# Gathered expert rows: products ahead of the preceding pair's sums, searches in four pieces, six row slots in place of eight

## The chip, the cores and the metric

The kernel runs on one core of a Trainium2 chip. The core has TensorE (PE, matrix products), VectorE (DVE), ScalarE (ACT), GpSimd (POOL) and SyncE (SP), each with an instruction queue of its own, and 16 DMA engines that they share. The metric is the device time of one execution in microseconds (us).

## What is computed

One layer of an encoder for 1024 tokens of width 1024, in float32: three mixers side by side (retention, gated unit, window attention), their merge, then a retrieval over 16384 experts (PEER), then a gated input embedding. The change lies in the retrieval and its surroundings. For a block of 128 tokens:

```python
q = (xt @ wq).reshape(T, PEER_HEADS, 2, PEER_QDIM // 2)          # 8 heads, two halves of 128
s = jnp.einsum('thpc,hpkc->thpk', q, kf)                         # 128 scores for each half
s1, i1 = lax.top_k(s[:, :, 0], 16)
s2, i2 = lax.top_k(s[:, :, 1], 16)
cand_s = s1[..., :, None] + s2[..., None, :]                     # 256 pairs
top_s, sel = lax.top_k(cand_s.reshape(T, PEER_HEADS, 256), 16)
eid = ...                                                        # i1 * 128 + i2 of the 16 chosen
gate = jax.nn.softmax(top_s, axis=-1)
act = jax.nn.gelu(jnp.einsum('thkd,td->thk', u_tab[eid], xt))
return jnp.einsum('thk,thkd->td', gate * act, v_tab[eid])
```

Each token picks 8 x 16 = 128 experts, and for each it needs one row u (1024 floats) and one row v (1024 floats). The kernel holds u and v side by side in one table, so an expert is a row of 8 KB.

## The kernel before

Two earlier stages (keys and branches) compute the mixers. The late stage, `late_stage` from line 969, merges them, projects, searches and retrieves. Tokens sit on the 128 partitions, one tile of 128 tokens at a time, 8 tiles. A "row" r of the code is one of the 1024 combinations of tile, head and chosen expert (8 x 8 x 16). For each row r, GpSimd issues one indirect DMA (`row`, lines 1186 to 1199) that fetches, for each of the 128 tokens, its own 8 KB table row: 1 MB in all. The tile `rows` in SBUF has SLOTS = 8 slots, and row r goes to slot r % 8. So GpSimd waits before gather r until row r - 8 has been summed.

What is done with a row:
- the product (`dot`, lines 1561 to 1569): VectorE multiplies u by the normalized input and adds up, one number per token;
- the weight (`weights`, line 1418): ScalarE applies GELU to the two products of a pair and multiplies by the gates; for rows of TensorE it also builds a diagonal matrix (line 1431);
- the sum (`weigh`): the v half times the weight is added to the tile's sum. Odd rows, and the even rows with r % 8 = 6, go to TensorE (`on_tensor`, line 824; product with the diagonal matrix, line 1297); the other even rows, 3 of 8, go to VectorE (line 1578).

The order of the work is written out ahead of time by the class `Plan` (line 838). It divides the late stage into slots of time, each with a list of jobs, and every engine runs through the slots in order. From the slot `first` on, each slot takes one pair of rows, 512 pairs in all. In slot s VectorE does first the merge jobs of slot s - 1, then the sums of pair s - 1 (which need ScalarE's weights), then the two products of pair s, then at the end of a tile the joining of the two sums (`finish`), and then the pieces of the searches that are planned for this slot. ScalarE does the evacuations of the jobs of slot s - 1 and then the weights of pair s. TensorE does its sums of pair s - 1 and then the jobs of slot s: projections of the next group of tiles, spread over the slots by their estimated times. They are there until tile 5 begins, and thin out as the groups of tiles end.

The searches for head q (the tile's heads in order) are planned by `searches` (line 950) in three pieces: both key searches (slot 3 of the group of 8 pairs that belongs to head q - 2), the search over the 256 pairs (slot 4) and the choice of experts (slot 6). One search (`top16`) is made of MAX8, FIND_INDEX8 and MATCH_REPLACE8 instructions. ScalarE converts indices (`convert`) in the slot after the pair search and scales the gates (`share`) in the slot after the choice. SP loads the scores of head q into one of two buffers in the slot in which head q - 2 has its pair search (line 1150).

Of the kernel before, what the change touches and what calls it, by code (L numbers as in the profile page):

```python
# [25 lines left out]
T = S // P  # L26
# [11 lines left out]
NSEL = PH * TOPK  # L38
# [7 lines left out]


FIRST = 1
SLOTS = 8


class Semaphores:
# [771 lines left out]
def on_tensor(r):  # L824

    return r % 2 == 1 or r % 8 == 6
# [11 lines left out]
class Plan:  # L838
# [111 lines left out]
    def searches(self):  # L950

        self.order = [(t, h) for t in range(T) for h in range(PH)]
        self.parts, self.part_slot = [[] for _ in range(self.n_slots)], {}
        ready = lambda q: self.of["scored", self.order[q][0], self.order[q][1] // 2].slot + 1

        def put(slot, q, part):
            assert slot >= ready(q), (slot, q, ready(q))
            self.parts[slot].append((q, part))
            self.part_slot[q, part] = slot

        for q in range(2):
            for part in range(3):
                put(self.first - 2 + (q + part + 1) // 2, q, part)
        for q in range(2, T * PH):
            for part, after in enumerate((3, 4, 6)):
                put(self.first + (q - 2) * HEAD_PAIRS + after, q, part)


def late_stage(nc, A, R, X):


    plan = Plan()
    with ExitStack() as ctx:
# [3 lines left out]
        K = max(len(g) for g in GROUPS)  # L977
        rows = sb("rows", [P, SLOTS, 2 * D])
        ring_rest = sb("ring", [P, RING - 2, CHUNK])
# [9 lines left out]
        s_in = sb("s_in", [P, 2, 2, PK])  # L989
        hot = sb("hot", [P, TOPK, 2, TOPK])  # L990
        top, top_at, top_f = sb("top", [P, 2, TOPK]), sb("top_at", [P, 2, TOPK], U32), sb("top_f", [P, 2, TOPK])
# [33 lines left out]
        xn_in, acc_in = [sem(f"xn{n}_in") for n in range(2)], [sem(f"acc{n}_in") for n in range(2)]  # L1025
        row_in = [sem(f"row{n}_in") for n in range(SLOTS)]
        pp_in, out_done = sem("pp_in"), sem("out_done")
# [24 lines left out]
        def pair_of(s):  # L1052

            g = s - plan.first
            return g if 0 <= g < PAIRS else None

        @block.sync
        def _(sp):
# [84 lines left out]
            chunks_at, scores_at, normed_at = ([[] for _ in range(plan.n_slots)] for _ in range(3))  # L1143
# [3 lines left out]
            for n in range(RING, len(plan.chunks)):  # L1147
                chunks_at[plan.last_job[n - RING].slot].append(n)
            for q, (t, h) in enumerate(plan.order):
                scores_at[max(plan.part_slot[q - 2, 1] if q > 1 else 0, plan.of["scored", t, h // 2].slot)].append(q)  # L1150
            for s in range(plan.n_slots):
                for g in range(len(GROUPS)):
                    for n in range(2, UNITS):
# [22 lines left out]
                for t in range(T):  # L1176
                    after = s - plan.first - (t + 1) * NSEL // 2
# [6 lines left out]
        @block.gpsimd  # L1184
        def _(pool):
            def row(r):

                c, n = divmod(r, TOPK)
                if n == 0:
                    pool.wait_ge(chosen, c + 1)  # L1190
                    pool.tensor_copy(at[:, c % 2, :], expert[:, c % 3, :]).then_inc(at_ready, 1)  # L1191
                    pool.wait_ge(at_ready, c + 1)
                if r >= SLOTS:
                    if on_tensor(r - SLOTS):
                        pool.wait_ge(acc2_done, n_pe(r - SLOTS) + 1)
                    else:
                        pool.wait_ge(acc_done, n_dve(r - SLOTS) + 1)
                pool.indirect_dma_start(out=rows[:, r % SLOTS, :], out_offset=None, in_=A["peer_uv"],  # L1198
                                        in_offset=bass.IndirectOffsetOnAxis(ap=at[:, c % 2, n:n + 1], axis=0)).then_inc(row_in[r % SLOTS], 16)

            for r in range(T * NSEL):
                row(r)
            for k in range(SLOTS):
                pool.wait_ge(row_in[k], T * NSEL // SLOTS * 16)

        @block.tensor
        def _(pe):
# [106 lines left out]
        def _(act):  # L1314
# [14 lines left out]
            def norm(g, i):  # L1329

                k = sum(len(group) for group in GROUPS[:g]) + i
                freed_pb(act, plan.of["out", g, 1, i].pb[0])
                wait(act, rms_ready, k)
                act.activation(xt[:, i, :], merged[:, i, :], ACT.Square, accum_out=rms[:, 0:1]).then_inc(rms_done, 1)
                act.dma_start(X["h"][GROUPS[g][i]], merged[:, i, :]).then_inc(h_out[i], 16)
                act.wait_ge(rms_done, k + 1)
                wait(act, xs_ready, k)
                act.activation(rms[:, 1:2], rms[:, 0:1], ACT.Sqrt, scale=1.0 / D, bias=R["eps"][:]).then_inc(rms_ready, 1)
# [60 lines left out]
            def convert(q):  # L1399

                act.wait_ge(parts_ready, q + 1)
                act.copy(part_f[:], part_u[:])
                act.mul(top_f[:, 0, :], top_at[:, 0, :], float(PK))
                act.copy(top_f[:, 1, :], top_at[:, 1, :]).then_inc(converted, 1)

            def exponentials(q):
                act.wait_ge(best_ready, q + 1)
                act.mul(total[:, q % 2, 0:1], best[:, q % 2, 0:1], -1.0).then_inc(neg_ready, 1)
                act.wait_ge(neg_ready, q + 1)
                act.activation(soft[:, q % 2, :], best[:, q % 2, :], ACT.Exp, bias=total[:, q % 2, 0:1], scale=1.0, accum_out=total[:, q % 2, 1:2]).then_inc(exp_ready, 1)  # L1410
                act.wait_ge(exp_ready, q + 1)
# [30 lines left out]
            for s in range(plan.n_slots):  # L1442
                if s % 8 == 0:
                    order.turn()
                for job in plan.at[s - 1] if s else ():
                    if job.kind in programs:
                        programs[job.kind](job)
                for g, i in norms_at[s]:
                    norm(g, i)
                for q, part in plan.parts[s - 1] if s else ():  # L1450
                    if part == 1:
                        convert(q)
                        exponentials(q)
                    if part == 2:
                        share(q)
                if pair_of(s) is not None:
                    weights(pair_of(s))
# [4 lines left out]
        def _(dve):  # L1462
# [60 lines left out]
            def top16(scores, values, where):  # L1523

                for k in range(2):
                    eight = slice(8 * k, 8 * k + 8)
                    order(dve.max(values[:, eight], scores))
                    order(dve.max_index(where[:, eight], values[:, eight], scores))
                    if k == 0:
                        order(dve.match_replace(out=scores, in_to_replace=values[:, eight], in_values=scores, imm_value=-3e38))  # L1530

            def search_keys(q):
                dve.wait_ge(scores_in[q % 2], (q // 2 + 1) * 16)
                wait(dve, converted, q)
                top16(s_in[:, q % 2, 0, :], top[:, 0, :], top_at[:, 0, :])
                top16(s_in[:, q % 2, 1, :], top[:, 1, :], top_at[:, 1, :])

            def search_pairs(q):
                tt(grid(cand[:]), top[:, 0, :].unsqueeze(2).to_broadcast(square), top[:, 1, :].unsqueeze(1).to_broadcast(square), ALU.add).then_inc(searched, 1)
# [21 lines left out]
            def dot(r):  # L1561

                t, n = r // NSEL, r % TOPK
                if r % NSEL == 0:
                    dve.wait_ge(xn_in[t % 2], (t // 2 + 1) * 16)
                dve.wait_ge(row_in[r % SLOTS], (r // SLOTS + 1) * 16)
                u = rows[:, r % SLOTS, 0:D]
                dve.scalar_tensor_tensor(out=u, in0=u, scalar=1.0, in1=xn[:, t % 2, :], op0=ALU.mult, op1=ALU.mult,  # L1568
                                         accum_out=dots[:, n:n + 1]).then_inc(dot_done, 1)
# [23 lines left out]
            for s in range(plan.n_slots):  # L1593
                order.turn()
                for g, i in scales_at[s]:
                    scale(g, i)
                for job in plan.at[s - 1] if s else ():
                    if job.kind in programs:
                        programs[job.kind](job)
                g = pair_of(s - 1)  # L1600
                if g is not None:
                    for r in (2 * g, 2 * g + 1):
                        if not on_tensor(r):
                            weigh(r)
                if pair_of(s) is not None:
                    dot(2 * pair_of(s))
                    dot(2 * pair_of(s) + 1)
                if g is not None and (2 * g + 2) % NSEL == 0:
                    finish(2 * g // NSEL)
                for t in range(T):  # L1610
                    if s == plan.of["pgate", t, 1].slot + 2:
                        output(t)
                for q, part in plan.parts[s]:
                    (search_keys, search_pairs, choose)[part](q)


SPILLS = {"xnt": [T, P, DC * P], "v": [T, P, RW], "kt": [T, P, RW], "yt": [T, P, 3 * RW], "pp": [T, P, D], "h": [T, P, D], "xn": [T, P, D],
# [105 lines left out]
```

## Time and profile before

| | |
|---|---|
| time, median of 3 runs (lowest to highest) | 4180.28 us (4174.69 to 4190.34) |
| the profiled execution's own time | 4184.72 us |
| its span | 4182.7 us |
| PE, DVE, ACT, POOL busy | 3192.3, 2681.3, 1374.7, 1374.6 us |
| gathers (DMA_INDIRECT) | 1024 of 1 MB, POOL busy 1353.3 us |
| products on DVE (L1568) | 1024, 1221 ns each |
| sums on DVE (L1578) | 384, 1285 ns each |
| sums on PE (L1297) | 2560 instructions, 730 ns each |
| queue of the gathers (q0) | 1073.81 MB, 64.6% of 16 engines over the span |
| granted TensorE clock, mean | 0.875 |

The span is that of one profiled execution. An engine's busy time leaves out waits and the issuing of DMAs. The idle time before an instruction is put down to whatever released it last.

### The profile page before, as it was taken

Reading aid. Unit: us, or ns where it says so; the run is one execution under the profiler, and the core shown is the slowest. Engines: PE = TensorE matmul, PEld = TensorE weight load, DVE = VectorE, ACT = ScalarE, POOL = GpSimd, SP = SyncE. Lnnn points to the kernel's source line nnn. Section 1 sums busy time; section 2 is a strip of 40 time slices with the busy share of each in tenths; the row PEclk is TensorE's granted clock in tenths of the full one; section 3 lists DMA queues with packets and bytes.
Section 4 is the critical chain, followed back from the end, with each engine's and each line's share of the span. In section 5 each row is a group of like instructions: output and inputs, shape, how many; then the busy total and the mean of one; then the engine's idle time right before and its main releaser. Section 6 shows DMA issues by size and latency. Waiting matters only on the chain. (4 is left out here: it accounts for less than half of the span.)

```text
span 4182.7 us, 30983 instructions
## 1 busy us (share of the span) xinstructions
PE 3192.3 (76%) x7816; PEld 1436.7 (34%) x7816; DVE 2681.3 (64%) x5254; ACT 1374.7 (33%) x3570; POOL 1374.6 (33%) x1092
## 2 busy tenths in 40 slices
PE   8979999897898889877777776788565566566566
PEld 4535555444333334333233332333222222222222
DVE  3344555214577567676677777767878887887884
ACT  3313333112344343333333433333333333333332
POOL 0000000002344334443444344434445454554452
PEclk9989999798999999988898888988878878878877
DMA  4330010357899989998999899989999999998996
GB/s 167 108 127 30 33 42 29 143 231 306 344 405 397 348 333 398 413 394 315 363 383 380 350 387 374 395 324 382 390 356 393 397 405 345 402 399 338 397 395 269
DMA packets 212916, 1295.14 MB, mean 310 GB/s; under 512 B 24608, under 2 KB 38176, under 8 KB 69408
## 3 DMA queue, kind: packets, MB, share of 16 engines
q0 software_dynamic: 147456, 1073.81, 64.6%
q1 hardware_dynamic: 59552, 207.15, 13.3%
q10 hardware_dynamic: 5760, 12.59, 0.8%
q8 instruction: 47, 0.77, 0.1%
q14 instruction: 101, 0.83, 0.0%
HBM read 1253.60 MB, written 39.85 MB: 309 GB/s over the span
## 5 line engine op out<-in xcount | busy, mean ns | idle before, releaser
L1297 PE MATMUL l_acc<-l_rows,l_diag 128*128 128x512 f32 x2560 | 1498.7, 730 | 860.8 <-ACT l_diag L1431 846.0
L1198 POOL DMA_INDIRECT l_rows<-in_peer_uv,l_at x1024 | 1353.3, 1322 | 1774.0 <-DVE l_acc L1578 861.3
L1568 DVE SCALAR_TENSOR_TENSOR l_rows<-l_rows,l_xn 128x1024 f32<-128x1024 f32 x1024 | 1209.4, 1221 | 30.8 <-DMA l_rows<-in_peer_uv,l_at 16.9
L1297 PEld LDWEIGHTS l_acc<-l_rows,l_diag 128*128 128x128 f32 x2560 | 548.7, 227 | 1742.8 <-ACT l_diag L1431 1168.9
L1578 DVE SCALAR_TENSOR_TENSOR l_acc<-l_rows,l_wts,l_acc 128x1024 f32<-128x1024 f32 x384 | 493.3, 1285 | 611.6 <-ACT l_wts L1427 568.8
L1423 ACT ACTIVATE l_dots<-l_dots 128x2 f32<-128x2 f32 x512 | 104.1, 203 | 1367.5 <-DVE l_rows L1568 1365.5
L1191 POOL CAST l_at<-l_expert 128x16 uint32<-128x16 f32 x64 | 21.1, 330 | 982.2 <-DVE l_expert L1554 981.9
L117 PE MATMUL l_pa<-all_ring,l_xt 128*128 128x512 f32 x656 | 294.7, 600 | 9.0 <-DMA l_xt<-kept_xnt 8.5
L1427 ACT ACTIVATE l_wts<-l_dots,l_gates 128x1 f32<-128x1 f32 x1024 | 293.5, 287 | 16.8
L117 PE MATMUL l_pa<-l_ring,l_xt 128*128 128x512 f32 x624 | 284.0, 607 | 14.8 <-DMA l_xt<-kept_xnt 9.0
L1431 ACT ACTIVATE l_diag<-all_ident,l_wts 128x128 f32<-128x128 f32 x640 | 256.9, 401 | 21.1
L117 PE MATMUL b_p<-mix_w_branches,b_xnt 128*128 128x512 f32 x384 | 191.4, 657 | 21.4 <-DMA b_gain<-in_att_q_norm 18.0
L117 PEld LDWEIGHTS l_pa<-all_ring,l_xt 128*128 128x128 f32 x656 | 126.3, 194 | 166.1 <-issue 157.2
L117 PEld LDWEIGHTS l_pa<-l_ring,l_xt 128*128 128x128 f32 x624 | 121.7, 196 | 167.2 <-issue 166.8
L1423 ACT ACT_TABLE_LOAD x114 | 146.3, 1283 | 97.8 <-DVE l_rows L1568 96.7
L117 PE MATMUL l_pb<-l_ring,l_yt 128*128 128x512 f32 x320 | 146.9, 609 | 0.0
L117 PE MATMUL l_pb<-all_ring,l_yt 128*128 128x512 f32 x320 | 145.5, 604 | 0.0
L117 PEld LDWEIGHTS b_p<-mix_w_branches,b_xnt 128*128 128x128 f32 x384 | 79.7, 213 | 124.5 <-issue 95.0
L117 PE MATMUL l_pa<-l_wg,l_ht 128*128 128x512 f32 x256 | 117.4, 613 | 3.9 <-issue 3.9
L117 PE MATMUL b_p<-b_w_last,b_xnt 128*128 128x512 f32 x256 | 112.3, 592 | 0.0
L1321 ACT ACTIVATE l_sgk<-l_pa 128x512 f32<-128x512 f32 x48 | 28.7, 597 | 242.5 <-PE l_pa L117 242.5
L707 DVE COPY b_pt<-b_p 128x384 f32<-128x384 f32 x64 | 35.7, 557 | 110.4 <-PE b_p L537 103.2
(241 smaller groups left out, 2787.8 us busy)
## 6 DMA issues: line engine op xcount, KB each, us to landing
l_ring<-in_w_late SPq DMA_DIRECT2D x44, 1024.0 KB, 9.9
all_ring<-in_w_late SPq DMA_DIRECT2D x44, 1024.0 KB, 8.3
l_rows<-in_peer_uv,l_at POOLq DMA_INDIRECT x1024
l_yt<-kept_yt SPq DMA_DIRECT2D x48, 256.0 KB
kept_s<-l_yt ACTq DMA_DIRECT2D x32, 256.0 KB
l_s_in<-kept_s SPq DMA_DIRECT2D x64, 128.0 KB
mix_w_branches<-in_w_branches_kept SPq DMA_DIRECT2D x8, 768.0 KB
kept_yt<-b_yt SPq DMA_DIRECT2D x8, 768.0 KB, 3.6
```

The source lines that it names most:

```text
L117: last = pe.matmul(out, lhsT, rhs, start=(n == 0), stop=(n == len(pairs) - 1))
L707: ring(dve, dve.tensor_copy(pt[:, n % 2, :], (p7, p6)[n % 2][:, 0:WIN]), Z["pt_ready"], t * AH + n + 1)
L1191: pool.tensor_copy(at[:, c % 2, :], expert[:, c % 3, :]).then_inc(at_ready, 1)
L1198: pool.indirect_dma_start(out=rows[:, r % SLOTS, :], out_offset=None, in_=A["peer_uv"], in_offset=bass.IndirectOffsetOnAxis(ap=at[:, c % 2 ...
L1297: ins = pe.matmul(acc2[:, hs], diag[n_pe(r) % DIAGS][:], rows[:, r % SLOTS, D + half * HB:D + (half + 1) * HB], start=first, stop=last)
L1321: act.activation(sg(job.i), pa[job.pa[0] % 2][:], ACT.Sigmoid).then_inc(pa_free[job.pa[0] % 2], 1)
L1423: act.activation(dots[:, n:n + 2], dots[:, n:n + 2], ACT.Gelu).then_inc(act_done, 1)
L1427: ins = act.mul(wts[:, m:m + 1], dots[:, m:m + 1], gates[:, c % 3, m:m + 1])
L1431: act.mul(diag[n_pe(r) % DIAGS][:], R["ident"][:], wts[:, m:m + 1]).then_inc(diag_ready, 1)
L1568: dve.scalar_tensor_tensor(out=u, in0=u, scalar=1.0, in1=xn[:, t % 2, :], op0=ALU.mult, op1=ALU.mult, accum_out=dots[:, n:n + 1]).then_inc ...
L1578: dve.scalar_tensor_tensor(out=acc[:, t % 2, :], in0=rows[:, r % SLOTS, D:2 * D], scalar=wts[:, n:n + 1], in1=acc[:, t % 2, :], op0=ALU.mu ...
```

## The change

Three edits in the late stage. SLOTS is 6 in place of 8. VectorE runs the two products of pair s ahead of the sums of pair s - 1. The searches are planned in four pieces, the two key searches apart: slots 3, 4, 5 (pair search) and 7 (choice); the slots of ScalarE's conversions and of SP's load follow. The final waits of GpSimd are counted anew, since 1024 isn't a multiple of 6.

```diff
-SLOTS = 8
+SLOTS = 6
@@ searches
         for q in range(2):
-            for part in range(3):
-                put(self.first - 2 + (q + part + 1) // 2, q, part)
+            for part, after in enumerate((-2, -2, -2, -1)):
+                put(self.first + after + q, q, part)
         for q in range(2, T * PH):
-            for part, after in enumerate((3, 4, 6)):
+            for part, after in enumerate((3, 4, 5, 7)):
                 put(self.first + (q - 2) * HEAD_PAIRS + after, q, part)
@@ SP
-                scores_at[max(plan.part_slot[q - 2, 1] if q > 1 else 0, ...
+                scores_at[max(plan.part_slot[q - 2, 2] if q > 1 else 0, ...
@@ GpSimd
             for k in range(SLOTS):
-                pool.wait_ge(row_in[k], T * NSEL // SLOTS * 16)
+                pool.wait_ge(row_in[k], len(range(k, T * NSEL, SLOTS)) * 16)
@@ ScalarE
-                    if part == 1:
+                    if part == 2:
                         convert(q)
                         exponentials(q)
-                    if part == 2:
+                    if part == 3:
                         share(q)
@@ VectorE
-            def search_keys(q):
+            def search_keys(q, half):
                 dve.wait_ge(scores_in[q % 2], (q // 2 + 1) * 16)
                 wait(dve, converted, q)
-                top16(s_in[:, q % 2, 0, :], top[:, 0, :], top_at[:, 0, :])
-                top16(s_in[:, q % 2, 1, :], top[:, 1, :], top_at[:, 1, :])
+                top16(s_in[:, q % 2, half, :], top[:, half, :], top_at[:, half, :])
@@ VectorE, the slots
+                if pair_of(s) is not None:
+                    dot(2 * pair_of(s))
+                    dot(2 * pair_of(s) + 1)
                 g = pair_of(s - 1)
                 if g is not None:
                     for r in (2 * g, 2 * g + 1):
                         if not on_tensor(r):
                             weigh(r)
-                if pair_of(s) is not None:
-                    dot(2 * pair_of(s))
-                    dot(2 * pair_of(s) + 1)
                 if g is not None and (2 * g + 2) % NSEL == 0:
                     finish(2 * g // NSEL)
@@
                 for q, part in plan.parts[s]:
-                    (search_keys, search_pairs, choose)[part](q)
+                    if part < 2:
+                        search_keys(q, part)
+                    else:
+                        (search_pairs, choose)[part - 2](q)
```

## Rows read from the trace of the kernel before

**Rows 1.** The page: busy time by engine, and GB/s in 40 equal slices.

```profile
PE 3192.3 (76%) x7816; PEld 1436.7 (34%) x7816; DVE 2681.3 (64%) x5254; ACT 1374.7 (33%) x3570; POOL 1374.6 (33%) x1092
...
GB/s 167 108 127 30 33 42 29 143 231 306 344 405 397 348 333 398 413 394 315 363 383 380 350 387 374 395 324 382 390 356 393 397 405 345 402 399 338 397 395 269
```

**Rows 2.** Four stretches, gathers alone: length, POOL busy (count), TensorE clock, DMA share, GB/s.

```profile
990.00:1800.00 810.00, 310.25 (x234) 0.94 0.95 381
1800.00:2600.00 800.00, 319.13 (x244) 0.88 0.94 367
2600.00:3400.00 800.00, 369.68 (x276) 0.83 0.96 379
3400.00:4140.00 740.00, 348.58 (x266) 0.80 0.96 385
```

**Rows 3.** First stretch, all engines: PE, PEld, DVE, ACT, POOL busy, clock, DMA, GB/s.

```profile
990.00:1800.00 810.00, 697.46 (x1704) 313.94 (x1704) 538.36 (x1055) 309.06 (x782) 314.38 (x248) 0.94 0.95 381
```

**Rows 4.** Waits of the whole run: us in total, times, longest us.

```profile
POOL l_rows L1198 <- DVE l_acc L1578: 861.3, 275, 9.2
POOL l_rows L1198 <- PE l_acc L1297: 770.8, 343, 21.5
...
DVE l_acc L1578 <- ACT l_wts L1427: 568.8, 237, 20.1
...
DVE l_rows L1568 <- DMA l_rows<-in_peer_uv,l_at: 16.9, 15, 2.4
```

**Rows 5.** Timeline, two pairs without a search: start, duration, instruction, idle time before it.

```profile
3000.75 1.29 DVE L1578 SCALAR_TENSOR_TENSOR l_acc<-l_rows,l_wts,l_acc 128x1024 f32<-128x1024 f32 x1 [1.22 <-ACT l_wts L1427]
3001.96 1.22 DVE L1568 SCALAR_TENSOR_TENSOR l_rows<-l_rows,l_xn 128x1024 f32<-128x1024 f32 x1
...
3004.24 0.09 DVE L1568 DVE_READ_ACCUMULATOR l_rows<-l_rows,l_xn 128x1 f32 x1
...
3005.55 1.28 DVE L1578 SCALAR_TENSOR_TENSOR l_acc<-l_rows,l_wts,l_acc 128x1024 f32<-128x1024 f32 x1 [1.22 <-ACT l_wts L1427]
...
3010.39 1.28 DVE L1578 SCALAR_TENSOR_TENSOR l_acc<-l_rows,l_wts,l_acc 128x1024 f32<-128x1024 f32 x1 [1.22 <-ACT l_wts L1427]
...
3011.95 1.67 POOL L1198 DMA_INDIRECT l_rows<-in_peer_uv,l_at  x1 [0.73 <-DVE l_acc L1578]
```

**Rows 6.** Timeline around a key search and the pair search after it.

```profile
3013.93 0.29 DVE L1527 MAX8 l_top<-l_s_in 128x8 f32<-128x128 f32 x1
...
3017.80 1.23 DVE L1568 SCALAR_TENSOR_TENSOR l_rows<-l_rows,l_xn 128x1024 f32<-128x1024 f32 x1 [0.23 <-DVEq L89]
...
3020.10 0.42 DVE L1539 TENSOR_TENSOR l_hot<-l_top 128x256 f32<-128x256 f32 x1
...
3023.27 0.17 DVE L1545 TENSOR_SCALAR l_part_u<-l_best_at 128x16 uint32<-128x16 uint32 x1
```

**Rows 7.** First pair, a later pair, and gathers and products counted until then.

```profile
982.85 1.08 POOL L1198 DMA_INDIRECT l_rows<-in_peer_uv,l_at  x1 [0.28 <-POOL l_at L1191]
...
990.84 1.23 DVE L1568 SCALAR_TENSOR_TENSOR l_rows<-l_rows,l_xn 128x1024 f32<-128x1024 f32 x1 [1.21 <-DMA l_rows<-in_peer_uv,l_at]
...
993.18 1.23 DVE L1568 SCALAR_TENSOR_TENSOR l_rows<-l_rows,l_xn 128x1024 f32<-128x1024 f32 x1 [1.11 <-DMA l_rows<-in_peer_uv,l_at]
...
3317.48 1.57 POOL L1198 DMA_INDIRECT l_rows<-in_peer_uv,l_at  x1 [3.21 <-PE l_acc L1297]
...
3328.05 1.23 DVE L1568 SCALAR_TENSOR_TENSOR l_rows<-l_rows,l_xn 128x1024 f32<-128x1024 f32 x1 [0.23 <-DMA l_rows<-in_peer_uv,l_at]
...
980.00:3317.00 2337.00, 962.80 (x726) 0.89 0.95 375
...
980.00:3328.00 2348.00, 860.46 (x1454) 0.89 0.95 375
```

**Rows 8.** A pair with more gathers queued ahead of it: first issue, second product.

```profile
4077.91 0.94 POOL L1198 DMA_INDIRECT l_rows<-in_peer_uv,l_at  x1 [0.30 <-issue]
...
4089.49 1.23 DVE L1568 SCALAR_TENSOR_TENSOR l_rows<-l_rows,l_xn 128x1024 f32<-128x1024 f32 x1 [1.27 <-DMA l_rows<-in_peer_uv,l_at]
```

More of the change, by code:

```diff
@@ L1149, in _ @@
             for q, (t, h) in enumerate(plan.order):
-                scores_at[max(plan.part_slot[q - 2, 1] if q > 1 else 0, plan.of["scored", t, h // 2].slot)].append(q)
+                scores_at[max(plan.part_slot[q - 2, 2] if q > 1 else 0, plan.of["scored", t, h // 2].slot)].append(q)
             for s in range(plan.n_slots):
```

## The prediction

> **What bounds the kernel now.** I read the page first [rows 1], then the gathering stage in four stretches [rows 2, 3], then the waits [rows 4], then one piece of the timeline [rows 5]. The first gather is issued at 982.9 us and the four stretches reach to 4140. All three edits lie inside them, so the 983 us ahead and the 40 us behind are left as they are.
>
> The four stretches [rows 2] hold 234, 244, 276 and 266 gathers, so 117, 122, 138 and 133 pairs of rows. A pair takes 810/117 = 6.92, 800/122 = 6.56, 800/138 = 5.80 and 740/133 = 5.56 us. The DMA engines are 94 to 96% busy all along, which looks like the bound. The waits say otherwise [rows 4]: VectorE waits for a gathered row 16.9 us in total, but 568.8 us for ScalarE's weights, and GpSimd stands still for 861.3 + 770.8 us until a slot comes free. So the rows lie ready, the slots are full, and those who consume set the pace. Each step of that loop is in [rows 5]: weighted sum at 3000.75, two products from 3001.96 to 3004.33 (2.37 us), 1.22 us of nothing until ScalarE's weights are there, next sum at 3005.55. That is 4.80 us a pair. The searches come on top [rows 6]: 3.87 us for both key searches (3013.93 to the next product at 3017.80), 3.34 us for the pair search (3020.10 to 3023.44), and the choice, once in 8 pairs. In the first stretch the projections are there too (PE 697 of 810 us busy [rows 3]); ScalarE has to wait for them before it gives weights (the wait for weights is 568.8/237 = 2.4 us on average and 20.1 at most).
>
> **The change part by part.**
>
> *Products ahead of the sums.* Nothing is added or removed on VectorE; the two products of pair g+1 now run before the sum of pair g. The 1.22 us of ScalarE's latency disappears behind 2.37 us of products. Taken alone this is worth up to the 568.8 us of the wait, but the DMA engines come next. A pair moved 381 x 6.92 = 2.64 MB in the first stretch, and 2.41, 2.20 and 2.14 MB in the others. At 405 GB/s, a rate that slices of both halves of the stage reach [rows 1], that is 6.51, 5.94, 5.43 and 5.29 us, so 117 x 0.41 + 122 x 0.62 + 138 x 0.37 + 133 x 0.27 = 211 us at most. The price is that a row which VectorE sums is let go later. It was 1.22 + 1.28 us after its pair's products; now the whole next pair's products come between, then 1.28 us of sum. While rows lie ready this costs nothing.
>
> *Six slots in place of eight.* A slot holds one gathered row, so the ring holds three pairs, not four. The cover that hid the first edit's price is gone, and the loop closes. Let E(g) be the end of the products of pair g. The sum of pair g ends at E(g+1) + 1.28. Only then is the gather into the slot of row 2g issued (0.28 us after the sum at 3010.39 ended, [rows 5]; I take 0.3), and the next gather stands behind it on GpSimd's queue, whether or not TensorE has let its slot go. From the first issue of a pair until the product of its second row can start is the flight, F. Then comes one product with its accumulator read, 1.27 us. So
>
> E(g+3) = E(g+1) + 1.28 + 0.3 + F + 1.27, and a pair takes half of 2.85 + F.
>
> With four pairs in the ring and the old order it was four pairs in 1.22 + 1.28 + 0.3 + F + 1.27, which bound nothing. The new loop is broken at every fourth pair, whose rows both go to TensorE and are let go earlier. But that helps the even pairs alone: the odd ones still follow one another, and the order on VectorE ties the two together.
>
> F: the first pair of all, on empty queues, was issued at 982.85. Its first product could start at 990.84 (7.99 us, for one row alone), its second at 993.18: 10.33 us. A pair in the middle (gather 727 of the run, 726 issued before it, and products 727 and 728, of which the second waited) was issued at 3317.48 and its second product began at 3328.05: 10.57 us [rows 7]. With more queued it took 4077.91 to 4089.49, 11.6 us [rows 8]. These pairs were late enough to be waited for; most others came unseen and may have been quicker, and with fewer slots less is queued. So F lies between 7.99 and 11.6; I take 9.9, a little under the two nearest rows. A pair then takes (2.85 + 9.9)/2 = 6.38 us in the last stretch. Earlier the projection weights share the DMA engines: 0.50, 0.27 and 0.06 MB a pair above the last stretch, at 405 GB/s 1.2, 0.66 and 0.15 us, and one pair's worth falls into each loop of two pairs. That makes 6.98, 6.71 and 6.45 us for the other three. Against before:
> 117 x 0.06 + 122 x 0.15 + 138 x 0.65 + 133 x 0.82 = 7 + 18 + 90 + 109 = 224 us more.
> At F = 7.99 (6.51 by the DMA floor, 5.94 likewise, 5.49 and 5.42 us) it is 117 x 0.41 + 122 x 0.62 + 138 x 0.31 + 133 x 0.14 = 185 us less. At 11.6 every pair takes 0.85 us more than at 9.9, so 224 + 434 = 660 us more. That end is of a full queue, which six slots can hardly build; 10.57 makes 224 + 171 = 395.
>
> The Trainium skill, "DMA: Bandwidth & Descriptors", section "Anatomy of one DMA — SWDGE (gpsimd) path", gives a DMA of this path about 2.0 us plus its bytes over 436 GB/s. For two gathers of 1 MB one behind the other that is an estimate of 6.8 us for F and of (2.85 + 6.8)/2 = 4.8 us a pair: the ring would not bind, and the change would bring the whole 211 us of the DMA floor. The trace does not bear it out: one gather alone on empty queues took 7.99 us until its use, where the page has 4.4.
>
> *Searches in four pieces.* The same instructions; the heaviest slot falls from 2.37 + 1.21 + 3.87 to 2.37 + 1.21 + 3.34 = 6.9 us, and that slot with the one ahead of it (half of the key searches, 1.9) holds 12.4 us. A loop of 2 x 6.38 = 12.8 us has room for them: 0 us. Without that cover, in a loop bound by VectorE, the edit is worth the restart of 0.23 us [rows 6], 64 times, 15 us either way. The choice of experts comes one slot later and is still seven slots ahead of its first gather. ScalarE's conversion and shares move one slot. So does SP's load of scores, where the search sets its slot (14 slots ahead of its use), and the chunk loads behind it on SP's queue wait for jobs of the same slot anyway. Before the first gather VectorE's order is the same: 0 us.
>
> Sum: the profiled execution took 4184.7 us (span 4182.7). 4184.7 + 224 = 4409; the median of the runs is 4.4 us lower than that execution, so 4404, and I say 4400 us.
>
> **The rivals.**
>
> *Faster: ScalarE's wait goes and the ring holds.* It decides for this if F is under 2 x 5.56 - 2.85 = 8.3 us. For it: 95% busy may be packets in a queue that six slots thin out, and 568.8 us of wait are there to be had. Against it: 10.33 us on empty queues, where no queueing is left to lose. The floor allows 211 us (3970); F = 7.99 makes 3995, and half of the 211 makes 4075, which I take. Chance 0.18, with 0.04 of it for the page's 3970.
>
> *No difference.* If F is 9.0, a pair takes 6.53, 6.26, 6.00 and 5.93 us. The first two stretches gain 117 x 0.39 + 122 x 0.30 = 82 us, because VectorE runs on where it had been stuck behind ScalarE, and the last two lose 138 x 0.20 + 133 x 0.37 = 77. That is 4175 us. Chance 0.08.
>
> *Slower by much more.* TensorE lets its rows go late behind a projection (GpSimd's longest wait for it was 21.5 us [rows 4]), and with three pairs in the ring nothing bridges that, so both causes add up. With 0.3 us for each of the 510 pairs: 4400 + 153 = 4550 us. Chance 0.13.
>
> **How the numbers follow.** The forecast has 0.61, by itself from 4270 (F 9.4) to 4510 (F 10.33). What a measurement of this kernel can tell from no change is 0.5%, 21 us. Faster 0.19 (the fast case and a part of the middle one), same 0.07, slower 0.74. The range, 4150 to 4520, leaves out most of the fast case and the larger half of the slowest.
>
> **What would show it.** In the changed profile VectorE's wait for ScalarE's weights should be almost gone, and its wait for gathered rows should rise from 16.9 us to several hundred. GpSimd's wait should be mostly for VectorE's sums. The last stretch should show 6.4 us a pair, and DMA 0.96 x 5.56/6.38 = 84% busy. The forecast is wrong if VectorE still doesn't wait for rows, or if F is 8 us. If the first two stretches gain much, I have misjudged how much of their time was ScalarE's block.

## The result

The changed kernel takes 4431.4 us (median of 4 runs, 4417.97 to 4439.02), the kernel before 4183.3 in the same series. The ratio is 1.0591, with a 95% interval of 1.0557 to 1.0624: 5.9% slower. The forecast was 4400 us, in a range of 4150 to 4520, by a circle in which the late sum holds back the gathers. The profiled execution took 4428.9 us, its span is 4426.7.

### The profile page after: what moved, and what is told of

Read it like the earlier page. It is cut to its first block and busy times, and to the rows that moved or that the text cites. A ratio compares the mean times of both kernels' runs of the same rounds, so it can differ in the third digit from the quotient of the medians.

```text
span 4426.7 us, 31094 instructions
## 1 busy us (share of the span) xinstructions
PE 3288.8 (74%) x7816; PEld 1464.6 (33%) x7816; DVE 2708.3 (61%) x5254; ACT 1381.3 (31%) x3574; POOL 1140.7 (26%) x1092
## 5 line engine op out<-in xcount | busy, mean ns | idle before, releaser
L1297 PE MATMUL l_acc<-l_rows,l_diag 128*128 128x512 f32 x2560 | 1588.1, 766 | 1001.7 <-ACT l_diag L1431 975.6
L1567 DVE SCALAR_TENSOR_TENSOR l_rows<-l_rows,l_xn 128x1024 f32<-128x1024 f32 x1024 | 1243.7, 1225 | 889.2 <-DMA l_rows<-in_peer_uv,l_at 840.0
L1198 POOL DMA_INDIRECT l_rows<-in_peer_uv,l_at x1024 | 1125.7, 1099 | 2256.3 <-DVE l_acc L1577 1746.4
L1297 PEld LDWEIGHTS l_acc<-l_rows,l_diag 128*128 128x128 f32 x2560 | 570.3, 237 | 1944.0 <-ACT l_diag L1431 1366.4
L1577 DVE SCALAR_TENSOR_TENSOR l_acc<-l_rows,l_wts,l_acc 128x1024 f32<-128x1024 f32 x384 | 491.6, 1280 | 42.1 <-ACT l_wts L1427 42.1
```

What stands on the lines that cost most here:

```text
L1297: ins = pe.matmul(acc2[:, hs], diag[n_pe(r) % DIAGS][:], rows[:, r % SLOTS, D + half * HB:D + (half + 1) * HB], start=first, stop=last)
L1577: dve.scalar_tensor_tensor(out=acc[:, t % 2, :], in0=rows[:, r % SLOTS, D:2 * D], scalar=wts[:, n:n + 1], in1=acc[:, t % 2, :], op0=ALU.mu ...
```

## The profile after

First the page of the changed kernel: busy time by engine, and GB/s in 40 slices (answers to [rows 1]).

```profile
PE 3288.8 (74%) x7816; PEld 1464.6 (33%) x7816; DVE 2708.3 (61%) x5254; ACT 1381.3 (31%) x3574; POOL 1140.7 (26%) x1092
...
GB/s 162 110 107 40 31 36 40 229 201 336 370 377 377 345 375 381 362 315 359 358 367 351 359 356 350 338 338 354 338 340 344 337 347 342 341 340 339 344 343 223
```

The work is the same. From the twelfth slice on the rate of the transfers is lower than before in most slices, and from the 26th on it is flat at about 340 GB/s but for the last: they look like transfers that wait for something regular. The same four stretches as in [rows 2], gathers alone:

```profile
990.00:1800.00 810.00, 241.47 (x223) 0.93 0.93 365
1800.00:2600.00 800.00, 255.47 (x235) 0.87 0.91 352
2600.00:3400.00 800.00, 273.96 (x248) 0.81 0.91 345
3400.00:4140.00 740.00, 261.63 (x236) 0.74 0.90 341
```

A pair takes 810/111.5 = 7.26, 800/117.5 = 6.81, 800/124 = 6.45 and 740/118 = 6.27 us, where it was 6.92, 6.56, 5.80 and 5.56. The waits of the changed kernel (answers to [rows 4]):

```profile
POOL l_rows L1198 <- DVE l_acc L1577: 1746.4, 378, 11.6
...
DVE l_rows L1567 <- DMA l_rows<-in_peer_uv,l_at: 840.0, 553, 7.1
...
POOL l_rows L1198 <- PE l_acc L1297: 353.1, 188, 21.5
...
DVE l_acc L1577 <- ACT l_wts L1427: 42.1, 11, 18.4
```

VectorE's wait for ScalarE's weights fell from 568.8 us to 42.1, as the new order promises. Its wait for gathered rows rose from 16.9 us to 840.0. GpSimd waits twice as long for VectorE's sums, 1746.4 us, and less than half as long for TensorE's, 353.1. This fits a circle: the sum waits for the products, the products for the rows, the rows for the slot, the slot for the sum.

One turn of it in the timeline of the changed kernel, GpSimd first and then VectorE. Up to 3700 us there are 806 gathers and 1604/2 = 802 products, so the gather at 3706.50 is number 807, and the product at 3712.79 is its own. The last fence has 1 us windows of GpSimd's gathers; the two numbers at the end of a line are the busy share of the DMA engines and GB/s.

```profile
3706.50 1.75 POOL L1198 DMA_INDIRECT l_rows<-in_peer_uv,l_at  x1 [8.16 <-DVE l_acc L1577]
3708.56 0.94 POOL L1198 DMA_INDIRECT l_rows<-in_peer_uv,l_at  x1 [0.30 <-issue]
3711.35 0.94 POOL L1198 DMA_INDIRECT l_rows<-in_peer_uv,l_at  x1 [1.85 <-DVE l_acc L1577]
3712.59 0.94 POOL L1198 DMA_INDIRECT l_rows<-in_peer_uv,l_at  x1 [0.30 <-issue]
3718.86 0.93 POOL L1198 DMA_INDIRECT l_rows<-in_peer_uv,l_at  x1 [5.33 <-DVE l_acc L1577]
```

```profile
3701.36 1.23 DVE L1567 SCALAR_TENSOR_TENSOR l_rows<-l_rows,l_xn 128x1024 f32<-128x1024 f32 x1 [2.65 <-DMA l_rows<-in_peer_uv,l_at]
...
3703.80 1.22 DVE L1567 SCALAR_TENSOR_TENSOR l_rows<-l_rows,l_xn 128x1024 f32<-128x1024 f32 x1 [1.21 <-DMA l_rows<-in_peer_uv,l_at]
...
3704.95 1.28 DVE L1577 SCALAR_TENSOR_TENSOR l_acc<-l_rows,l_wts,l_acc 128x1024 f32<-128x1024 f32 x1
3706.22 1.23 DVE L1567 SCALAR_TENSOR_TENSOR l_rows<-l_rows,l_xn 128x1024 f32<-128x1024 f32 x1
...
3708.65 1.22 DVE L1567 SCALAR_TENSOR_TENSOR l_rows<-l_rows,l_xn 128x1024 f32<-128x1024 f32 x1 [1.20 <-DMA l_rows<-in_peer_uv,l_at]
...
3709.80 1.28 DVE L1577 SCALAR_TENSOR_TENSOR l_acc<-l_rows,l_wts,l_acc 128x1024 f32<-128x1024 f32 x1
3712.79 1.23 DVE L1567 SCALAR_TENSOR_TENSOR l_rows<-l_rows,l_xn 128x1024 f32<-128x1024 f32 x1 [1.71 <-DMA l_rows<-in_peer_uv,l_at]
...
3716.16 1.22 DVE L1567 SCALAR_TENSOR_TENSOR l_rows<-l_rows,l_xn 128x1024 f32<-128x1024 f32 x1 [2.14 <-DMA l_rows<-in_peer_uv,l_at]
...
3717.31 1.28 DVE L1577 SCALAR_TENSOR_TENSOR l_acc<-l_rows,l_wts,l_acc 128x1024 f32<-128x1024 f32 x1
```

```profile
0.00:3700.00 3700.00, 882.04 (x806) 0.87 0.75 287
...
0.00:3700.00 3700.00, 978.63 (x1604) 0.87 0.75 287
```

```profile
3706.00:3707.00 1.00, 0.50 (x1) 0.50 0.60 254
3707.00:3708.00 1.00, 1.00 (x1) 0.50 0.12 49
3708.00:3709.00 1.00, 0.69 (x2) 0.50 0.27 41
3709.00:3710.00 1.00, 0.50 (x1) 1.00 0.71 164
```

Read it as the formula has it. The sum ends at 3704.95 + 1.28 = 3706.23, the gather is issued 0.27 us later, its pair's second product begins at 3716.16 (F = 9.66 us), the sum behind it (of the pair before) runs from 3717.31 to 3718.59, and the gather that it lets go is issued 0.27 us after that. From 3706.50 to 3718.86 it is 12.36 us for two pairs, 6.18 us a pair; the last stretch has 6.27. The engines ran dry in between (12 and 27% busy from 3707 to 3709), because no gather had been issued since 3697.41.

One turn might be an exception. Counted over the timeline of the whole last stretch (118 pairs), the second product of 88 pairs waited for its row, and the median F of these is 9.68 us. VectorE lets go of the first slot of 89 pairs, and 74 of those gathers start within 0.5 us of the end of the sum. From the second product of a pair to that of the pair after next it is 12.54 us, as mean and as median, and 80% of these times lie between 11.2 and 13.8. Single pairs are less even: by their place in a head's eight pairs they take 5.24 to 7.76 us on average, and the longest is the one behind the choice of experts.

## The experiments

All times are medians of 4 runs, beside runs of the kernel before on the same chip (4177 to 4185 us); ratios are to those, with their 95% intervals. Differences in us between two changed kernels of different series can be off by a few us. "New order" is the products ahead of the sums; "pieces" are the pieces of the searches. The last column is the time of a pair from 3400 to 3900 us, as 500 us over half the gathers in that stretch.

| order | pieces | slots | us | ratio | last stretch |
|---|---|---|---|---|---|
| old | 3 | 8 (the kernel before) | 4183 | 1 | 5.68 |
| old | 4 | 8 | 4153.3 | 0.9928 (0.9906 to 0.9950) | 5.59 |
| old | 3 | 6 | 4357.1 | 1.0404 (1.0373 to 1.0435) | 6.02 |
| new | 3 | 8 | 4047.8 | 0.9696 (0.9674 to 0.9719) | 5.29 |
| new | 4 | 8 | 3987.4 | 0.9538 (0.9518 to 0.9557) | 5.10 |
| new | 4 | 7 | 4141.1 | 0.9905 (0.9888 to 0.9921) | 5.71 |
| new | 3 | 6 | 4491.2 | 1.0740 (1.0711 to 1.0769) | 6.41 |
| new | 4 | 6 (the changed kernel) | 4431.4 | 1.0591 (1.0557 to 1.0624) | 6.25 |
| between | 4 | 8 | 4031.6 | 0.9629 (0.9613 to 0.9645) | 5.08 |
| between | 4 | 6 | 4299.1 | 1.0276 (1.0255 to 1.0296) | 5.85 |

**Eight slots again.** The changed kernel with one line put back.

```diff
-SLOTS = 6
+SLOTS = 8
```

> The changed kernel with eight slots again: new order and four pieces, ring of four pairs. My theory (the ring closes only with three pairs): four pairs then take one pair plus 1.28 + 0.27 + 9.7 + 1.2 us, 4.2 us a pair, which binds nothing, and the DMA engines come next: 3970 to 4100 us, I say 4050, with the wait for rows under 200 us. Rival (the new order itself is what costs, since VectorE stands before a product with the sum queued behind it): it stays above 4300 us. Second rival (the slots are worth the same with either order): about 4350.

3987.4 us, so 444 us lie in the two slots, and without them the change would be 4.6% faster. It beats both kernels, and it was the fastest of all that I ran. It is inside the range I gave, but its wait for rows is 263.4 us, where I had said under 200. Its waits (two lines), and its gathers from 2600 to 3900 us:

```profile
DVE l_rows L1567 <- DMA l_rows<-in_peer_uv,l_at: 263.4, 219, 5.6
...
DVE l_acc L1577 <- ACT l_wts L1427: 115.7, 41, 28.1
```

```profile
2600.00:3400.00 800.00, 348.98 (x298) 0.85 0.99 405
3400.00:3900.00 500.00, 230.32 (x196) 0.82 1.00 417
```

The DMA engines are 99 and 100% busy and carry 405 and 417 GB/s, the rate I had taken as the floor and a little more. So in these stretches the transfers have hardly any room left; with the sum still earlier (below) a pair takes 5.08 us from 3400 to 3900 in place of 5.10. VectorE is not far from its own bound either, 655 of 800 us busy from 2600 to 3400, and no run shortens the transfers with eight slots, so that they alone set the time is not shown. Both rivals, that the new order itself costs (above 4300) and that the slots are worth the same with either order (4350), fell.

**Six slots, old order.** In the kernel before, SLOTS is 6 and the final waits are counted as in the changed kernel; nothing else.

```diff
-SLOTS = 8
+SLOTS = 6
```

> The kernel before with six slots and nothing else changed (only the final waits counted anew). My theory: with the sums ahead of the products, three pairs take 1.22 + 1.28 + 0.3 + 9.7 + 1.2 = 13.7 us, 4.6 us a pair, less than the 5.6 to 6.9 that a pair takes anyway; what is lost is only cover against late moments: 4190 to 4290 us, I say 4230. Rival (the slots alone cost it all): 4400 us or more.

4357.1 us: 174 us slower, over three times the 48 us that I expected and outside my range, and still not the 444 us of the new order (443 with three pieces, in the table). So the slots cost more when the sums come late, but they aren't free with the old order. Its waits:

```profile
POOL l_rows L1198 <- DVE l_acc L1578: 1053.9, 324, 9.2
POOL l_rows L1198 <- PE l_acc L1297: 831.9, 369, 21.4
DVE l_acc L1578 <- ACT l_wts L1427: 502.4, 234, 20.0
DVE l_rows L1568 <- DMA l_rows<-in_peer_uv,l_at: 243.5, 196, 6.4
```

Rows are waited for here too (243.5 us against 16.9), while the loop of the formula (13.7 us for three pairs) leaves a pair 1 us of room. The mean of a loop is not the whole cost. That the steps are not all alike and three pairs in the ring don't level them out is my reading; no run takes this 174 us apart.

**The sum between the two products.** The changed kernel with six and with eight slots.

```diff
                 if pair_of(s) is not None:
                     dot(2 * pair_of(s))
-                    dot(2 * pair_of(s) + 1)
                 g = pair_of(s - 1)
                 if g is not None:
                     for r in (2 * g, 2 * g + 1):
                         if not on_tensor(r):
                             weigh(r)
+                if pair_of(s) is not None:
+                    dot(2 * pair_of(s) + 1)
```

> The changed kernel (six slots, four pieces) with the sum of pair g between the two products of pair g+1. My theory: in the changed kernel the second row of a pair lands 2.4 to 3.4 us after the first, and the sum (1.28 us) fits in there; it then ends 1.6 us ahead of the pair's last product, not 1.28 us behind it. Two pairs take -1.6 + 0.27 + 9.7 + 1.2 = 9.6 us, 4.8 a pair, under the DMA floor: 4050 to 4200 us, I say 4120. Rival (TensorE's late rows or six slots as such set the time, not the sum's place): above 4300 us.

> Eight slots, four pieces, and the sum between the two products. With the new order eight slots reached 3987 us at 417 GB/s and all DMA engines busy at the end. My theory: that is the floor of the transfers, and a still earlier release brings nothing: 3960 to 4000 us. Rival (the first two stretches, at 397 GB/s, still lose time at late sums): 3940 or less. Second rival (the sum between waits for ScalarE's weights again, 1.22 us behind one product of 1.22): 4050.

With six slots 4299.1 us: 132 us less than the changed kernel, from the sum's place alone, and VectorE's work is the same. It goes the way the circle demands, but stops 180 us above what I expected, at the mark of the rival (above 4300) that six slots as such set the time. Both are there: the two slots cost 174 us with the sum ahead of the products (three pieces), 268 (4299.1 against 4031.6) with it between them, and 444 with it behind. What grows with the sum's place is the circle; the rest is not explained by it. The timeline shows both, first where it works, then where it doesn't:

```profile
3720.44 1.23 DVE L1567 SCALAR_TENSOR_TENSOR l_rows<-l_rows,l_xn 128x1024 f32<-128x1024 f32 x1 [1.21 <-DMA l_rows<-in_peer_uv,l_at]
...
3725.32 1.23 DVE L1567 SCALAR_TENSOR_TENSOR l_rows<-l_rows,l_xn 128x1024 f32<-128x1024 f32 x1 [1.21 <-DMA l_rows<-in_peer_uv,l_at]
...
3730.77 1.23 DVE L1567 SCALAR_TENSOR_TENSOR l_rows<-l_rows,l_xn 128x1024 f32<-128x1024 f32 x1 [1.72 <-DMA l_rows<-in_peer_uv,l_at]
```

```profile
3701.60 0.94 POOL L1198 DMA_INDIRECT l_rows<-in_peer_uv,l_at  x1 [0.30 <-issue]
...
3707.19 1.19 POOL L1198 DMA_INDIRECT l_rows<-in_peer_uv,l_at  x1 [4.44 <-DVE l_acc L1577]
```

From 3720.44 to 3725.32 a pair takes 4.88 us, close to the 4.8 of the formula, though it is a single pair and the stretch has 5.85. Before that a pair search stood on VectorE from 3700.41 to 3703.75; the next sum began only at 3705.14, and GpSimd issued nothing from 3701.60 to 3707.19.

With eight slots the place brings nothing more (4031.6, 44 us slower than the new order), and the second rival named there was right: the wait for ScalarE's weights is back at 273.2 us, where the new order has 115.7. One product of 1.22 us leaves no room over a latency of 1.22 us.

**One more product on VectorE, ahead of the sum or behind it.** The changed kernel, with a product of 1.22 us on scratch data in each slot. (The scratch tiles, and their clearing once ahead of the slots, are left out here.)

```diff
+            def extra(s):
+                order(dve.scalar_tensor_tensor(out=junk[:], in0=junk[:], scalar=1.0, in1=gain[:], op0=ALU.mult, op1=ALU.mult, accum_out=junk_sum[:]))
                     dot(2 * pair_of(s) + 1)
+                    extra(s)        # ahead of the sum; in the other kernel behind weigh(r)
```

> The changed kernel (six slots) with one more product of 1.22 us on scratch data in each slot, between the pair's products and the sum of the preceding pair; it computes nothing that is used. My theory (the loop over three pairs closes through the end of the sum): every sum ends 1.3 us later, so two pairs take 1.3 us more, 0.65 us x 512 = 330 us: 4760 us. Rival (VectorE is idle 840 us anyway, so work of 1.3 us is hidden wherever it stands): the same as the run with the product behind the sum. Second rival (VectorE's load is what counts): 512 x 1.3 = 670 us more in both places, 5100.

> The same additional product, but behind the sum of the preceding pair, ahead of the searches. My theory: the sum ends as early as before, VectorE has 840/512 = 1.6 us of idle time a pair behind it, and only slots with a search have none: 64 x 4 x 0.5 us = 130 us more, 4560 us, at least 150 us under the run with the product ahead. Rivals: as told there, both the same, at 4430 to 4600 or at 5100.

Ahead of the sum 4665.9 us, 234 more than the changed kernel; behind it 4585.1, 154 more. The same work costs 81 us more where it delays the sum. The sign is what the circle says, and neither rival's pair of numbers fits, but the difference is half of the least that I expected (150), and the one ahead cost 0.46 us a pair in place of 0.65. So the sum is not what holds up every pair.

**Seven slots.** `SLOTS = 7` in the changed kernel.

> The changed kernel with seven slots. The sum of an even row 2g now lets go of the slot for row 2g+7, the second row of its pair; the first goes to a slot that TensorE or an earlier sum has freed. My theory: then one gather and not two lies behind the sum's end, about 7 us in place of 9.7, so two pairs take 1.28 + 0.27 + 7 + 1.2 = 9.8 us, 4.9 a pair, which is under the DMA floor of 5.3; with less cover than eight: 4020 to 4150 us, I say 4090. Rival (each slot is worth the same, half of the 444 us between six and eight): 4210.

4141.1 us: of the 444 us between six and eight, 290 lie between six and seven and 154 between seven and eight. The first step is the larger, as one gather behind the sum in place of two would have it, and the rival (equal steps, 4210 us) fell; but the second step is larger than the 100 us that my 4090 left for it.

**Shorter rows.** The changed kernel with 6 KB rows (the host's table holds u and the first half of v; what is read in their place stands in the expectation).

```diff
+WIDTH = 1536
-                pool.indirect_dma_start(out=rows[:, r % SLOTS, :], ...
+                pool.indirect_dma_start(out=rows[:, r % SLOTS, 0:WIDTH], ...
```

> The changed kernel (six slots) with gathered rows of 6 KB in place of 8 (a table of u and the first half of v; TensorE reads that half twice and VectorE's sum reads columns 512 to 1535, so the same work is done on other data, and the output is not the retrieval's). My theory: two gathers in a row take 2 x 0.61 = 1.2 us less, so two pairs take 1.2 us less, 0.6 us x 512 = 310 us: 4120 us. Rival (the rate of the transfers sets the time): every pair is 1.2 us shorter, 620 us less, 3810 us. Second rival (the fixed part of the flight or VectorE's work sets it): 4380 or more.

4211.0 us, 220 less, 0.43 us a pair of the 0.6 that the loop gives, and far from the 1.2 that the rate of the transfers would give. The DMA engines were 78% busy in the last stretch and the pair took 5.81 us:

```profile
3400.00:3900.00 500.00, 187.80 (x172) 0.78 0.78 278
```

So the rate of the transfers does not set the time: the engines are a fifth idle, and the saving is about a third of what the rate would give. A shorter transfer still shortens the kernel, through the flight. Where the second product waited, the median F in the last stretch (3400 to 4140) is 8.97 us against 9.68, which is 0.7 us less and not the 1.2 that I had reckoned; so the saving, too, is smaller than forecast.

**Three pieces, in the changed kernel and with eight slots.** Both are the kernel before with the new order; `three_pieces_six` has six slots as well.

> The changed kernel with the searches in three pieces as before: new order and six slots alone. My theory as corrected by the runs (with three pairs in the ring every long slot of VectorE delays a sum and so the gathers behind it): the slot with both key searches (7.4 us) and the one with the pair search (6.9) lie side by side, 14.3 us where a loop has 12.4, so 1.9 us for each of 64 heads, 120 us more: 4550 us. Rival (what I predicted, the pieces are worth 0): 4420 to 4440 us.

> The kernel before with the new order and nothing else: eight slots, three pieces. My theory: the DMA engines bound it with four pieces (3987 us), and with four pairs in the ring a slot of 7.4 us is nearly covered: 3990 to 4030 us. Rival (the pieces bring with the new order at least what they bring alone, 29 us, and more): 4050 us or more.

4491.2 and 4047.8 us. The four pieces bring 60 us with the new order, with six slots (4491.2 to 4431.4) and with eight (4047.8 to 3987.4), and 29 us with the old one, from this run:

> The kernel before with the searches in four pieces and nothing else changed. My theory: the same instructions, worth 15 us either way: 4170 to 4200 us. Rival (long searches in one slot hold the sums and so the gathers, and cutting them frees them): 4100 us or less.

With six slots I had expected 120 us, with eight at most 43, and alone, with the old order, no more than 15. All three missed, and with eight slots it is the rivals that came close (4050 or more with the new order; with the old one 4153.3 lies between my 4170 and the rival's 4100).

**All sums on TensorE.** The changed kernel with

```diff
-    return r % 2 == 1 or r % 8 == 6
+    return r % NSEL != 0
```

> The changed kernel (six slots, new order, four pieces) with all sums on TensorE but the first of each tile, so that no slot waits for a sum of VectorE. My theory: a pair is then let go 3 to 5 us after its products, three pairs take 4 + 0.27 + 9.7 + 1.2 = 15.2 us, 5.1 a pair; in the last stretch I expect 5.5 to 5.8 us a pair where the changed kernel has 6.27. In the first two stretches TensorE, 85% busy, gets 1 us a pair more and gives that back. In all 4150 to 4300 us. Rival (six slots cost it wherever the sums are made): 6.1 us a pair or more in the last stretch, over 4350 us.

4289.2 us (1.0262, 1.0236 to 1.0288), and 740/130.5 = 5.67 us a pair in the last stretch, where the changed kernel has 6.27. Six slots remain, and VectorE's late sum is gone. Its first and last stretch, and two of its waits:

```profile
990.00:1800.00 810.00, 245.62 (x218) 0.98 0.91 355
...
3400.00:4140.00 740.00, 292.39 (x261) 0.93 0.96 379
```

```profile
POOL l_rows L1198 <- PE l_acc L1297: 1967.0, 855, 22.7
...
DVE l_rows L1567 <- DMA l_rows<-in_peer_uv,l_at: 1054.9, 652, 8.5
```

The circle is shorter, not gone: it now runs through TensorE's sums, and VectorE waits even more for rows than in the changed kernel (1054.9 us against 840.0). This edit also takes a sum of 1.28 us off VectorE in three pairs out of four, so by itself it does not tell the sum's lateness from VectorE's load; the run with the sum between the products does, where that load is the same. The first stretch is slower than in the changed kernel (218 gathers against 223). TensorE is 771 of 810 us busy there, against 678; that this is the cause is likely but not shown.

## Why the prediction was right, step by step

- *The bound of the kernel before* (rows ready, slots full, consumers set the pace): right. Taking most of the wait for the weights away (568.8 to 125.8 us) gave 130 us (4177.4 to 4047.8 in one series), with eight slots.
- *At most 211 us by the DMA floor*: right in kind. With eight slots the order alone gained 130 us of those 211, and with the four pieces it was 195; the DMA engines were 99 to 100% busy at the end. The rate I took, 405 GB/s, was a little low for the last stretch (417).
- *The loop over three pairs*: right, and shown in the timeline (12.36 us for two pairs, 12.54 on average in the last stretch) and by opening or shortening it in four ways: eight slots, the sum between, shorter rows, sums on TensorE. By stretch I had 6.98, 6.71, 6.45 and 6.38 us a pair, and measured were 7.26, 6.81, 6.45 and 6.27. The last two, where hardly anything but gathers is left, are within 2%; the first is 4% low.
- *The flight F*: taken as 9.9, and 9.68 us as the median in the last stretch, which makes (2.85 + 9.68)/2 = 6.27. But my reading of the row it came from was wrong. I called the first pair's 10.33 us (7.99 for its first row) a flight on empty queues. No gather was ahead of it, but the DMA engines were 97% busy with other transfers before it was issued (first line, 0 gathers) and 102% until its use:

```profile
979.00:982.80 3.80, 0.00 (x0) 1.00 0.97 386
983.00:991.00 8.00, 6.17 (x7) 0.59 1.02 407
```

In the turn above, on engines that were running dry, the first row took 6.29 us (3706.50 to 3712.79) and the pair 9.66. The last pair of the run, also met by idle engines, has the same two times. So "no queueing is left to lose" had no ground, though the rival still falls: some 0.7 us of the 10.33 could be lost, and it needed 2 us (F under 8.3). The estimates from the Trainium skill ("DMA: Bandwidth & Descriptors", section "Anatomy of one DMA — SWDGE (gpsimd) path"), 4.4 us for one gather and 6.8 for two, are too low for the gathers on idle engines as well.

- *What was left out*: I took the loop as a mean and let long slots of VectorE vanish in it. The old order with six slots (174 us where that mean gives little), the sum between (180 us over its expectation) and the timeline of 3700 to 3707 show that a search also delays a sum, and with three pairs in the ring the gathers behind it. The first stretch is 0.28 us a pair over the forecast; searches and projections are both there, and no run separates them.
- *The pieces, 0 us*: mis-sized. Cutting the searches brings 60 us with the new order (4491.2 to 4431.4 with six slots) and 29 us with the old one, where I had 15 at most. The 0 was the claim that the searches, once in four pieces, cost nothing on top of a loop of 12.8 us. No run takes them out altogether, but my reason, that two slots next to one another fit into a loop, looks at the mean again.
- *The busy share, 84%*: wrong. It is 90% in the last stretch. The bytes fell as forecast, from 385 to 341 GB/s, but the busy share did not fall in proportion: 0.96 goes with 385 GB/s, 0.90 with 341 and, with 6 KB rows, 0.78 with 278. So the busy share is no measure of the rate here.
- *The rivals*: "faster" would have needed F under 8.3 us; "much slower" asked for TensorE's late rows, and GpSimd's wait for TensorE halved instead.
- *How near it came*: the 31 us between 4400 and 4431 are, by stretch, 33 and 12 us more in the first two and 15 less in the last. That it is only 31 is in part luck. Step by step the measured 248 us are 174 for the two slots with the old order, 134 for the order with six slots, and 60 gained by the pieces; the sum had all of it from the loop and nothing for the first and the last of these. What is not luck is the time of a pair where gathers are alone, and the waits: 568.8 to 42.1 us for weights, 16.9 to 840.0 for rows.

## What to carry to other kernels

Work the ring out as a circle: from the release of a buffer through issue, flight, and use, to the next release, divided by how many turns are under way. If that comes near the step time, an order that hides a wait by releasing a buffer later can cost more than the wait: here it cost 134 us with three pairs in the ring and gained 130 with four. Busy DMA engines (94 to 96%) and hardly any wait for data (16.9 us) were both true of the kernel before; taking two buffers away and looking at the wait for data (243.5 us) said more than the busy share. And leave the ring more room than the mean asks for, since a long step, such as a search, delays the releases behind it: with the old order the mean left 1 us a pair, and two slots fewer still cost 174 us.

## What I had not expected of the hardware

- The transfers reached 417 GB/s in the kernel with eight slots and the new order, with all 16 DMA engines busy, over 500 us of gathers of 8 KB rows. No stretch of the kernel before was above 385, though single slices of 105 us reached 413 [rows 1].
- A pair of gathers onto DMA engines that were running dry took 9.66 us until its second row was used (3706.50 to 3716.16), hardly less than the 10.33 us of the first pair of the kernel before, on engines 97 to 102% busy. For the first row it was 6.29 against 7.99 us; the second gather was issued 2.06 us behind it, against 1.39.
- TensorE's granted clock was lower where it had fewer products to do. In the last stretch it was 0.80 in the kernel before [rows 2] with 755 matrix products, 0.74 in the changed one with 669, and 0.93 with all sums on TensorE and 1117. These are means of two levels: in the 1 us windows above it is 0.50 or 1.00, that is 1.2 or 2.4 GHz. In the changed kernel the matrix products of the sums took 766 ns on average against 730. GpSimd's wait for TensorE fell all the same (770.8 to 353.1 us), so no cost of it shows there.

```profile
3400.00:4140.00 740.00, 442.21 (x669) 159.35 (x668) 524.39 (x1030) 221.36 (x673) 264.71 (x251) 0.74 0.90 341
```
